# Two mixture-of-experts stages: router order, place of the wide lap, last step in stream order

## The reference, cut to what matters

```python
for l in range(DEPTH):                       # DEPTH = 2
    hc = modulate(rms_norm(xc, norm1_g[l]), mc[0], mc[1])      # and hs for the sample
    ...                                      # layer 0: even_mixer, layer 1: odd_mixer
    xc = xc + (mc[2] * oc).astype(xc.dtype)
    hc = modulate(rms_norm(xc, norm2_g[l]), mc[3], mc[4])
    xc = xc + (mc[5] * hier_moe(hc, *moe_args)).astype(xc.dtype)
y_prompt = rms_norm(xc, final_norm_g)        # y_sample from xs
```

## Time and profile before

| | |
|---|---|
| median of 3 runs | 1094.12 us (1092.83 to 1096.31) |
| the profiled execution | 1095.51 us |
| its span in the trace | 1093.6 us |
| PE busy | 958.8 us (88%) |
| DVE, ACT, POOL busy | 266.4, 196.6, 40.8 us |
| read from memory | 322.11 MB |
| mean granted clock of TensorE | 0.932 of full speed |
| chain that ended last | PE 73%, DMA 20%, DVE 3%, ACT 2% |

### The profile page before, as it was taken

The page is one execution under the profiler, slowest core; times in us unless marked ns, Lnnn a source line. Parts: engine busy times, 40 slices in busy tenths (PEclk is TensorE's granted clock), DMA queues, the critical chain, the costliest instruction groups (busy, mean ns, idle before and its releaser), DMA issues.

```text
span 1093.6 us, 14223 instructions
## 1 busy us (share of the span) xinstructions
PE 958.8 (88%) x6039; PEld 543.0 (50%) x6039; DVE 266.4 (24%) x697; ACT 196.6 (18%) x363; POOL 40.8 (4%) x74
## 2 busy tenths in 40 slices
PE   1799999989899998676699999999998999987763
PEld 0585555574566564443444444444445665644431
DVE  1110235640731212100213212223007321221002
ACT  3111121250211010000222022344102110100001
POOL 3000000111000000000000010000100000000000
PEclk9899999988799999888789999999997999998887
DMA  9999829995298999999964444124942979999991
GB/s 322 402 360 358 308 88 367 410 412 203 77 389 323 422 416 420 422 420 421 388 226 153 154 153 163 68 77 167 408 155 82 411 316 423 416 421 421 421 421 55
DMA packets 72119, 329.19 MB, mean 301 GB/s; under 512 B 5724, under 2 KB 6100, under 8 KB 47220
## 3 DMA queue, kind: packets, MB, share of 16 engines
q1 hardware_dynamic: 66228, 310.56, 71.3%
q0 software_dynamic: 5360, 16.49, 4.3%
q10 hardware_dynamic: 464, 1.18, 0.3%
HBM read 322.11 MB, written 6.09 MB: 300 GB/s over the span
## 4 chain that ended last, share of the span: by engine, by line
PE 73%; DMA 20%; DVE 3%; ACT 2%; issue 1%; SPq 1%; DVEq 0%; ACTq 0%
PE PS L648 70%; DMA ring<-in_moe_w_down 17%; DMA ring<-in_mod_w 3%; SPq L529 1%; PE PS L686 1%; ACT HT L1234 0%; PE PS L1164 0%; PE PS L964 0%; PE PS L969 0%; DVE X L1603 0%; PE PS L781 0%; ACT scratch L1227 0%; ACT scratch L1522 0%; DVE scratch L1812 0%; DVE scratch L1815 0%
## 5 line engine op out<-in xcount | busy, mean ns | idle before, releaser
L648 PE MATMUL PS<-ring,scratch 128*32 128x256 f32 (+4 forms) x2592 | 307.9, 485 | 63.5 <-DMA ring<-in_moe_w_gate 32.9
L648 PE MATMUL PS<-ring,HT 128*128 128x512 f32 x576 | 255.4, 600 | 2.5 <-ACT HT L1234 1.7
L648 PEld LDWEIGHTS PS<-ring,scratch 128*32 128x32 f32 (+2 forms) x2592 | 146.6, 132 | 220.4 <-issue 184.7
L648 PEld LDWEIGHTS PS<-ring,HT 128*128 128x128 f32 x576 | 109.4, 192 | 134.8 <-issue 130.5
L648 PE MATMUL PS<-scratch 128*128 128x512 f32 (+3 forms) x504 | 124.6, 431 | 4.4 <-issue 1.5
L648 PE MATMUL PS<-scratch,H 128*128 128x128 f32 x640 | 86.4, 292 | 6.9 <-DVE scratch L1943 6.9
L648 PEld LDWEIGHTS PS<-scratch 128*128 128x128 f32 (+2 forms) x504 | 59.9, 183 | 62.6 <-issue 56.1
L648 PEld LDWEIGHTS PS<-scratch,H 128*128 128x128 f32 x640 | 80.7, 205 | 14.4 <-issue 14.3
L2004 DVE TENSOR_TENSOR scratch<-PS,scratch 128x256 f32<-128x256 f32 x20 | 8.5, 425 | 276.9 <-ACT scratch L1409 276.9
L648 PE MATMUL PS<-ring,cpad 128*32 128x256 f32 x768 | 47.8, 402 | 16.6 <-DMA ring<-in_mod_w 16.6
L1409 ACT ACTIVATE scratch<-PS 128x256 f32<-128x256 f32 x20 | 7.7, 384 | 255.0 <-PE PS L648 255.0
(11 more groups left out here) (283 smaller groups left out, 656.7 us busy)
## 6 DMA issues: line engine op xcount, KB each, us to landing
ring<-in_moe_w_up SPq DMA_DIRECT2D x64, 1024.0 KB, 14.3
ring<-in_moe_w_down SPq DMA_DIRECT2D x64, 1024.0 KB, 14.4
ring<-in_moe_w_gate SPq DMA_DIRECT2D x56, 1024.0 KB, 15.1
ring<-in_mod_w SPq DMA_DIRECT2D x24, 2048.0 KB, 15.9
ring<-in_odd_w_in SPq DMA_DIRECT2D x12, 2048.0 KB, 13.7
ring<-in_even_w_in SPq DMA_DIRECT2D x7, 2048.0 KB, 16.2
ring<-in_odd_w_out SPq DMA_DIRECT2D x4, 2048.0 KB, 7.7
ring<-in_even_w_out SPq DMA_DIRECT2D x2, 2048.0 KB, 21.9
```

The costliest lines, as they stand in the source:

```text
L648: return nc.tensor.matmul(out, lhsT, rhs, start=start, stop=stop, skip_group_check=True, **kw)
```

## The change

It alters the order of work in both expert stages and leaves all sizes of the computation as they are.

```diff
-LAPS = ([("pairs", [("expert", n) for n in range(4)]), ("quad", [("rank", n) for n in range(4, 8)]),
-         ("pairs", [("rank", n) for n in range(4)])]
-        + [("quad", [("rank", n) for n in range(m, m + 4)]) for m in range(8, NSORT, 4)])
+def laps():
+    ...
+    return [fixed] + narrow[:4] + [wide] + narrow[4:]
+SHIFT_AT = (NSTEP - 3, NSTEP - 2)
+def split_down(item):
+    return item[2] == len(LAPS) - 1 and item[3] >= 4
...                                                    # SP
+                        if split_down(STREAM[n]):
+                            for u in range(4):
+                                at = SLOT // 4 * u
+                                sp.dma_start(ring[:, SLOT_OF[n], at:at + SLOT // 4].rearrange("p (a b) -> p a b", a=1),
+                                             down_rows(l, ids[u], j - 4)).then_inc(landed[SLOT_OF[n]], 16)
...                                                    # PE, project_out
-                pe.wait_ge(x_ready, 2 * n + 2)
-                turn_stream(1, X)
+                pe.wait_ge(x_half, l + 1)
+                for k in range(KT):
+                    if k == KT // 2:
+                        pe.wait_ge(x_ready, 2 * n + 2)
+                    mm = nc.tensor.transpose(PS[:, 2 + k // 4, P * (k % 4):P * (k % 4) + P], X[:, 1, P * k:P * k + P], ident)
+                    if k % 4 == 3:
+                        mm.then_inc(ht_half if k < 4 else ht_done, 1)
...                                                    # PE, moe
-                start_zero(0)
-                start_zero(1)
...
+                    if last:
+                        for j in range(2):
+                            arrived(pe, items[2][j])
+                            for half in range(2):
+                                mm = down_rows(half, j, sl[2][j])
+                                if j and not half:
+                                    mm.then_inc(down0_done, 1)
+                            mm.then_inc(used, 1)
+                        return
...
                 for i in range(NSTEP):
+                    if i == NSTEP - 1:
+                        rest()
                     step(i)
...
-                scatter((NSTEP - 1) % 2)
...
+                for s in range(S):
+                    scatter((NSTEP - 1) % 2, streams=[s]).then_inc(moe_done, 1)
...
-            logit_shift(1, 4)
...                                                    # DVE, moe_end
-                dve.wait_ge(branch_done, n // 2 + 1)
                 dve.wait_ge(gate_in, 32 * (n + 1))
+                dve.wait_ge(moe_done, 2 * (n // 2) + 1)
                 residual(n, 0)
+                dve.wait_ge(moe_done, 2 * (n // 2) + 2)
```

More of the change, by code:

```diff
@@ L61 @@
 MOD_BANK = {1: 7, 2: 7, 3: 3}
-LAPS = ([("pairs", [("expert", n) for n in range(4)]), ("quad", [("rank", n) for n in range(4, 8)]),
-         ("pairs", [("rank", n) for n in range(4)])]
-        + [("quad", [("rank", n) for n in range(m, m + 4)]) for m in range(8, NSORT, 4)])
+def laps():
+    fixed = ("pairs", [("expert", n) for n in range(NFIXED)])
+    wide = ("pairs", [("rank", n) for n in range(NWIDE)])
+    narrow = [("quad", [("rank", n) for n in range(m, m + 4)]) for m in range(NWIDE, NSORT, 4)]
+    return [fixed] + narrow[:4] + [wide] + narrow[4:]
+LAPS = laps()
 def lap_steps():
@@ L519, in _ @@
                         sp.wait_ge(order_ready, 2 * l + 1)
-                    ids = [v if how == "expert" else
-                           sp.value_load(ORDER[0:1, v:v + 1], min_val=NFIXED, max_val=NE - 1) for how, v in who]
+                    if lap == len(LAPS) - 1:
+                        sp.wait_ge(count_ready, l + 1)
+                        most = sp.value_load(CNT[0:1, 0:1], min_val=0, max_val=S * P)
+                        with sp.If(most > 0):
+                            ov = OV[l]
+                            sp.wait_ge(used, AT[("moe", l, lap, 0)])
+                            with sp.Fori(0, REST_ROUNDS) as r:
+                                with sp.Fori(0, NPAIR) as p:
+                                    for m in range(3):
+                                        sp.wait_ge(ov["used"], (r * NPAIR + p) * 3 + 1)
+                                        src = expert_source(l, m, p)
+                                        dst = ring[:, m, :].rearrange("p (a b) -> p a b", b=src.shape[2])
+                                        sp.dma_start(dst, src).then_inc(ov[f"in{m}"], 16)
+                            sp.wait_ge(ov["used"], REST_ROUNDS * NPAIR * 3 + 1)
+                    ids = {}
                     for j in range(RING):
@@ L991, in down, with down_rows, scatter @@
                     return mm
-                def scatter(par):
-                    for s in range(S):
+                def down_rows(half, j, place):
+                    for e in range(4):
+                        a = SLOT // 4 * e + BANK * half
+                        mm = matmul(PS[32 * e:32 * e + 32, 4 + half, :], ACTT[:, j, 32 * e:32 * e + 32],
+                                    ring[:, place, a:a + BANK], j == 0, j == 1)
+                    return mm
+                def scatter(par, first=False, streams=range(S)):
+                    for s in streams:
                         for half in range(2):
-                            mm = matmul(PS[:, 2 * s + half, :], WSELT[:, par, s, :], YG[:, half, :], False, False)
+                            mm = matmul(PS[:, 2 * s + half, :], WSELT[:, par, s, :], YG[:, half, :], first, False)
                     return mm
@@ L1016, in step @@
                         pe.wait_ge(wselt_ready, t)
-                        scatter(1 - par)
+                        scatter(1 - par, i == 1)
+                    if l == 0 and i in SHIFT_AT:
+                        logit_shift(1, SHIFT_AT.index(i), 4)
                     for x in items[1]:
@@ L1624, in mixer_end @@
                 dve.wait_ge(used, AT[item] + 1)
-                residual(n, 1)
+                for half in range(2):
+                    cols = slice(BANK * half, BANK * half + BANK)
+                    st.link(V.tensor_tensor(GATE[:, 1, cols], PS[:, 2 + half, :], GATE[:, 1, cols], ALU.mult))
+                    V.tensor_tensor(X[:, 1, cols], X[:, 1, cols], GATE[:, 1, cols], ALU.add)\
+                        .then_inc(x_ready if half else x_half, 1)
                 shift_h(0)
@@ L1841, in _ @@
                     .then_inc(attn_probs_ready, 1)
-            router_weights(0, 5)
+            router_weights(0)
+            for s in range(S):
+                keep_shift(0, s, 5)
             mixer_end(0, ("even_out", 1))
@@ L2011, in step @@
                     V.tensor_copy(YG[:, 0, :], PS[:, 4, :]).then_inc(yg0_ready, 1)
-                select(0)
-                rank()
-                shift_h(1)
-                order()
+                for s in range(S):
+                    st.mark(compare(PLACE[:, 0, :], s, (0,))[0])
+                st.wait()
+                for s in range(S):
+                    build(PLACE[:, 0, :], s, 0).then_inc(sel_ready, 1)
+                order()
+                shift_h(1)
+                weights()
@@ L2017, in moe @@
+                st.wait()
+                for s in range(S):
+                    st.mark(compare(PLACE[:, 0, :], s, (1,))[0])
+                st.wait()
+                for s in range(S):
+                    weigh(s, 0).then_inc(wsel_ready, 1)
                 dve.wait_ge(gather1_done, NSTEP * l + 1)
                 xg_half(1, 0).then_inc(xg1_ready, 1)
+                dve.wait_ge(wsel_ready, 2 * NSTEP * l + 2)
                 select(1)
                 place_sorted()
-                step(0)
@@ L2078, in _ @@
                 modulate(2, s)
-            router_weights(1, 4)
             def evac_odd(c):
```

350 lines of the change are left out of this document (185 added, 165 removed).

## The result

| | before | changed |
|---|---|---|
| runs in this comparison | 4 | 4 |
| median, us | 1093.47 (1091.97 to 1096.31) | 1075.98 (1071.74 to 1080.75) |
| ratio of times | | 0.9841 [0.9812, 0.9869] |
| the profiled execution, us | 1095.51 | 1071.74 |
| its span, us | 1093.6 | 1069.7 |

The changed kernel is faster by 17.5 us, inside the range and 2.5 us above the forecast of 1073.5. A later comparison of five rounds gave 0.9851 [0.983, 0.987] (experiment 12). The profiled execution is the fastest of its four, and that of the kernel before is 2.0 us slower than its median, so the span falls by 23.9 us, more than the medians do. Neither kernel has a trace of its median execution.

What follows compares the result with a forecast made beforehand. Each expert stage was taken as bound first by PE's steps, then by 174 us of DMA loads, then by its end. Terms -3.2, -0.5, -10.35 and -6.55 sum to -20.6, giving 1073.5 us, range 1065 to 1081.

Steps and rivals of the forecast that it cites:

- The router: Router ahead of step 0: without zero matmuls and with fewer sum records, step 0 starts 1.6 us earlier, -3.2 for two layers.
- Rival 1: Low clock at the stage ends, or a branch sticking out, takes back half the gains: 1078 to 1083 us; chance 0.17.
- The half turn: Router, stream 1 turned in halves: buys little, and the last logits come 0.5 us later.
- The order for SP: `ORDER` written earlier, SP's first load 5.9 us earlier: costed at nothing, since later blocks wait for PE's slots.
- Rival 2: Earlier order and four quads in a row close DMA's pause before the seam: 1063 to 1066 us; chance 0.10.
- The wide lap: Wide lap moved later, quads behind the seam: SP's slots no longer just in time, 0.25 us a layer, -0.5 in all.
- Rival 3: The moved wide lap starves DMA, 25 us in each layer at half clock: 1123 us; chance 0.03.
- The end of stage 0: Last landing to odd mixer in layer 0: split down, streams signalled singly, branch moved, earlier mixer start: -10.35, bounds -8.6 and -12.1.
- The branch: Moved before step 9, its 3.50 us stall fits under PE's 4.62 us wait for gate blocks, with 1.1 to spare.
- The end of stage 1: Last landing to the end in layer 1: shorter down, earlier residual, smaller last store: -6.55, bounds -5.3 and -7.3.
- Pieces of 0.5 MB: Last lap's down loads in small pieces: costed at nothing in a full queue; SP issues eight in 3.5 us.
- Rival 5: Small pieces do not overlap in the queue, 12 us more in each layer: 1097.5 us, a quarter of it 1079.5; chance 0.02.

Runs made afterwards that it cites:

- experiment 12: The changed kernel run again unaltered, on the chip of the later runs: 1076.63 us, ratio 0.9851 to the kernel before.
- experiment 7: The changed kernel with stream 1 added, turned and copied whole, not in halves: 1075.78 us, a single execution.
- experiment 3: The changed kernel with `ORDER` written late again, behind the weights of step 0: 1075.18 us, ratio 0.9819 to the kernel before.
- experiment 2: The kernel before with only the wide lap moved to sixth: 1095.55 us, ratio 0.9997 to the kernel before.
- experiment 1: The changed kernel with the wide lap back in its old third place: 1077.85 us, ratio 0.9847 to the kernel before.
- Experiment 8: The changed kernel with unused dummy matmuls in PE's waits at the end of each stage: 1066.93 us, ratio 0.975 to the kernel before.
- experiment 4: The changed kernel with whole 1 MB down blocks in the last lap: 1077.13 us, ratio 0.9845 to the kernel before.
- experiment 5: The changed kernel with a branch behind the last scatter again, over 75 matmuls that never run: 1082.8 us, a single execution.

## Why the prediction was right, and where it was not

The total was right, but by errors of both signs. The sum gave -20.6, and the same stretches in the two traces give -19.9. The medians give -17.5, 3.1 less than forecast; which stretches are longer in the executions near the median is not known, since those have no trace.

- **The router** was undersized: -3.2 forecast for both layers, -7.1 measured. The sums came as early as worked out: the copy to `PRE` 2.22 us sooner after the first turn in layer 0 where 2.25 less 0.5 was forecast, and 1.14 in layer 1. DVE's ranking costs 0.36 where 0.5 was counted. The step that failed is "I count 0.35 of this", for the gathers. From the first gather to step 0 it is 7.07/6.01 us, and it was 8.46/9.06. I had taken the rise of the clock to be tied to 6 us after the gathers begin. In the kernel before it came 6.7 and 8.0 us after the first gather, in the changed one 5.1 and 2.9. Layer 0 around the rise, before and changed:

```profile
297.39:304.05 6.66, 6.66 (x30) 6.28 (x31) 3.15 (x10) 0.14 (x1) 1.10 (x2) 0.50 0.29 76
304.15:305.85 1.70, 1.02 (x10) 0.81 (x9) 0.80 (x2) 0.99 (x3) 0.00 (x0) 1.00 1.06 431
```
```profile
291.47:296.50 5.03, 5.03 (x23) 5.03 (x24) 4.07 (x12) 0.00 (x0) 1.10 (x2) 0.50 0.61 207
296.60:298.54 1.94, 1.33 (x13) 1.12 (x12) 0.79 (x2) 1.15 (x3) 0.00 (x0) 1.00 0.99 391
```

Why it came sooner is not shown: no run puts the zero matmuls or the gathers in two pieces back. Layer 0's gain holds in every trace of this router (first turn to step 0 in 23.96 to 24.32 us, before 27.51). Layer 1's -3.82 is at the lucky end: the changed kernel has 23.66 there and the others 23.65 to 25.89, so the gain is 1.6 us in the worst of them. Rival 1's doubt on the router did not come true.
- **The half turn** was priced at 0.5 us and costs 0.2 (experiment 7).
- **The order for SP** was costed at nothing, and experiment 3 confirms it. I had expected a pause of 7 to 10 us before the seam and it is 5.0. The first load now leads step 0 by 6.1 us in place of 2.7, which is 3.5 more and not 4.3, since step 0 came earlier than forecast too; and the DMA engines are busy for 45.4 us of that window, where it was 43.2 before and 43.4 in experiment 3. Why they need 2 us more is not shown. Rival 2, that the pause closes, is refuted: it grew by 1.2 us.
- **The wide lap** was to bring 0.5. Alone it brings nothing (experiment 2), and in this kernel at most 1.1 and 0.3 (experiment 1), while seam to landing is 0.6 and 0.3 longer than before. The term had the right size, near nothing; its sign the runs do not tell. Its costs are covered as forecast: the wide steps take 20.1 and 20.2 us on the chain, under the 23.8 from which they would cost, and PE still idles 6.03 and 4.94 us before step 9, ended by DMA. One sign of being right, PE idle under 5 us there, is missed by that 6.03. Rival 3 is refuted.
- **The end of stage 0** was forecast at -10.35 and gave -8.6. The split down is right (-3.16 for -3.55). The step that failed is "now stream 0 is signalled after 1.83: 1.93": that is a scatter at the high clock. I had left the scatter's clock to rival 1, which priced it at 1.8. It takes 5.60 in place of 3.67, and the residual comes at 3.86, 1.93 late. Experiment 8 shows that it is the clock, since with PE kept busy and the clock at 1.00 the same scatter takes 3.67 and the residual comes at 2.06. That the split brings the low clock into the scatter is not shown: with whole blocks (experiment 4) the scatter is at full clock, but so it is with split blocks in layer 0 of experiments 1 and 5. The start of the mixer was better than forecast, -1.69 for -1.1; no run puts `logit_shift` back behind the stage, so this is read from the traces alone.
- **The branch** is off the path. Before step 9 the wait of 6.03 us ends with a landing, so the stall is hidden, whatever it is there. The prediction took from the Trainium skill ("Runtime: NRT & Kernel Launch", section on instruction fetch mechanics) that the branch would stall in its new place too; no trace shows whether it does.
- **The end of stage 1** was forecast at -6.55 and gave -5.04. Of this 0.9 is the last down, at the low clock (3.48 us) and not between the two, and 0.5 is the store. I had priced it by a store of 256 KB that landed in 2.4 us; the half store here takes 2.7, the whole one took 2.8, and DVE's scaling takes 2.61 us in three pieces where it took 2.48 in two:

```profile
out_y_sample<-scratch ACTq DMA_DIRECT2D x1, 256.0 KB, 2.7
```

- **Pieces of 0.5 MB** overlap in the queue: seam to last landing is 0.4 and 0.0 us longer than with whole blocks. Rival 5 is refuted. By the Trainium skill's rule of at least 1 MiB a transfer ("DMA: Bandwidth & Descriptors", section on measured bandwidth) the prediction's estimate was 3 us a stage; in this full queue the measurement does not bear it out. SP's issuing was mis-sized: its eight loads take 11.4 and 10.9 us and not 3.5, and 5.8 us of it are on the chain in layer 0, yet the last landing is no later for it.
- **Two slips in the working** change nothing: the terms of the end of stage 0 add up to an upper bound of 11.9 and not 12.1, and the time by which DMA needs the last wide slot is 55 in one place and 53 in another.

In short, rival 1's mechanism is real in one half of its places, for about 3 us, and the router made up for it. The forecast came out at the size it did because the two cancel, and that is luck.

## What to carry to other kernels

Read a wait that you shorten together with the clock behind it: the low clock can move from the matmul that you shortened into the next one, and give the gain back there. Look at more than one trace before you give such a stretch a size, since the same program had the low clock now here, now there. A few dummy matmuls in the waits at a stage's end, sized from the trace so that they end before the data lands, were worth more here (9.7 us) than most parts of the change. Where ring slots bound the prefetch, an earlier order is worth nothing; count from the event that frees the slot (here step 0 + 44.30 us in every kernel).

## What the runs showed of the hardware

- **The time of a run goes with its mean granted clock.** Runs of one kernel on one chip spread over 6 to 9 us. In experiment 12 they were 1073.08 at 0.945, 1076.47 at 0.940, 1076.63 and 1077.81 at 0.936, 1079.04 at 0.937; those of the kernel before beside it went from 1091.83 at 0.937 to 1098.33 at 0.929. The profiled execution of the changed kernel had 0.950, the highest of its four; what its further 4.1 us ahead of the router come from was not tried.
- **The clock fell while one-row matmuls ran.** The zero matmuls of the earlier trace rows keep PE busy from 285.59 to 291.37 with one row each. In the kernel before the granted clock is 1.00 up to 287.00, and 0.50 from 287.10 on, with PE busy throughout:

```profile
285.60:287.00 1.40, 1.40 (x5) 0.67 (x5) 1.23 (x10) 0.11 (x2) 0.00 (x0) 1.00 0.00 0
287.10:291.37 4.27, 4.27 (x7) 1.20 (x6) 4.10 (x18) 0.21 (x2) 0.00 (x0) 0.50 0.00 0
```

Whether the one row has to do with it was not tried.
- **A branch over a long skipped block cost time, one over a short block none**: 1 and 75 matmuls show no gap on PE, 600 one of 1.5 us in layer 0 (behind a slower scatter) and 3.3 in layer 1, each from one trace.
